# Another fixed order for every step of ScalarE and VectorE, and a Sqrt as the first activation

## What is computed

```
# first block, layer 0 (T = 16 meta tokens + 256)
proj = rmsnorm(h) @ w_in                        # latents q (3 tiles), kv (2), rotary key, gate (8 tiles)
q  = rmsnorm(q_lat)  @ w_uq ; kv = rmsnorm(kv_lat) @ w_ukv
y  = causal_attention(q, kv) * silu(gate)       # 8 heads; silu by tanh on the chip
h += y @ w_out
# layer 1: gated linear recurrence
u, gate = split(rmsnorm(h) @ w_in); uc = conv4(u)
r, i = sigmoid(uc @ w_rg + b), sigmoid(uc @ w_ig + b)
log_a = -8 * r * softplus(-lam); a = exp(log_a); b = sqrt(-expm1(2 log_a)) * i * uc
h += (scan(a, b) * silu(gate)) @ w_out ; x = rmsnorm(h)
# second block, layers 0 and 1: attention over tokens and over a memory, then a squared-ReLU MLP
x += concat(attention, memory_attention) @ w_out ; x += relu(rmsnorm(x) @ w_up)**2 @ w_down
return rmsnorm(x)
```

## Time and profile before

| | us |
|---|---|
| median of 3 runs | 815.59 (815.41 to 815.99) |
| span of the profiled execution | 814.4 |
| TensorE (PE) busy | 801.8, 98% |
| VectorE (DVE) busy | 602.5, 74% |
| ScalarE (ACT) busy | 550.7, 68% |
| granted TensorE clock, mean | 0.998 |

### The profile page before, as it was taken

How to read it: one execution, slowest core, us unless ns; L and a number is a source line. 1 busy time by engine, 2 the same in 40 slices (tenths; PEclk the granted TensorE clock), 3 DMA queues, 4 the chain that set the end, 5 groups by cost and what they waited for, 6 DMA issues and landing times.

```text
span 814.4 us, 14821 instructions
## 1 busy us (share of the span) xinstructions
PE 801.8 (98%) x5854; PEld 747.8 (92%) x5854; DVE 602.5 (74%) x1140; ACT 550.7 (68%) x1045; POOL 0.2 (0%) x4
## 2 busy tenths in 40 slices
PE   8999999999999999999999999999999999999997
PEld 8989899999999899988989999998899888888886
DVE  7999997989987995876657475866757667564664
ACT  7876876699977888767455465668866756553652
POOL 0000000000000000000000000000000000000000
PEclk9999999999999999999999999999999999999999
DMA  9533344665564544464837365444434657554451
GB/s 329 191 103 130 105 147 144 201 201 169 182 202 130 175 137 130 155 226 137 281 117 248 130 238 178 130 133 153 149 111 157 211 177 236 188 175 167 166 181 52
DMA packets 40676, 137.83 MB, mean 169 GB/s; under 512 B 4640, under 2 KB 6176, under 8 KB 40608
## 3 DMA queue, kind: packets, MB, share of 16 engines
q1 hardware_dynamic: 39600, 135.70, 50.0%
q10 hardware_dynamic: 1008, 1.20, 0.4%
HBM read 135.83 MB, written 1.05 MB: 168 GB/s over the span
## 4 chain that ended last, share of the span: by engine, by line
PE 88%; DVE 9%; ACT 1%; issue 1%; DMA 1%; ACTq 0%; DVEq 0%
PE bank L796 15%; PE bank L803 15%; PE bank L798 14%; PE bank L797 14%; PE bank L804 7%; PE bank L807 5%; PE bank L809 5%; PE bank L808 5%; DVE weights_lo L1753 2%; PE bank L1171 2%; DVE temp L1753 1%; DMA weights_raw<-stream_dram 1%; DVE arena L1753 1%; DVE operand L1753 1%; DVE temp L1756 1%
## 5 line engine op out<-in xcount | busy, mean ns | idle before, releaser
L1753 DVE TENSOR_TENSOR weights_lo<-weights_raw,weights_hi 128x1024 fp32r<-128x1024 f32 (+3 forms) x257 | 299.7, 1191 | 37.1 <-ACT weights_hi L1249 36.7
L796 PE MATMUL bank<-operand,weights_hi 128*128 128x256 f32 (+1 forms) x1092 | 313.5, 287 | 1.6 <-DVE weights_lo L1753 1.0
L798 PE MATMUL bank<-operand,weights_lo 128*128 128x256 f32 (+1 forms) x1092 | 309.5, 283 | 0.0
L797 PE MATMUL bank<-operand,weights_hi 128*128 128x256 f32 (+1 forms) x1092 | 309.1, 283 | 0.0
L1249 ACT ACTIVATE weights_hi<-weights_raw 128x1024 fp32r<-128x1024 f32 (+3 forms) x257 | 257.3, 1031 | 76.2 <-PE bank L798 34.6
L796 PEld LDWEIGHTS bank<-operand,weights_hi 128*128 128x128 f32 x1092 | 206.1, 189 | 7.6 <-issue 5.0
L798 PEld LDWEIGHTS bank<-operand,weights_lo 128*128 128x128 f32 x1092 | 206.2, 189 | 0.0
L797 PEld LDWEIGHTS bank<-operand,weights_hi 128*128 128x128 f32 x1092 | 205.8, 188 | 0.0
L803 PE MATMUL bank<-operand,weights_hi 128*128 128x512 f32 x512 | 180.1, 394 | 0.0
L804 PE MATMUL bank<-operand,weights_lo 128*128 128x256 f32 x512 | 143.6, 281 | 0.0
L803 PEld LDWEIGHTS bank<-operand,weights_hi 128*128 128x128 f32 x512 | 96.2, 188 | 21.3
(11 more groups left out here) (212 smaller groups left out, 791.8 us busy)
## 6 DMA issues: line engine op xcount, KB each, us to landing
weights_raw<-stream_dram SPq DMA_DIRECT2D x242, 512.0 KB, 4.3
weights_raw<-stream_dram SPq DMA_DIRECT2D x6, 384.0 KB, 3.5
temp<-memT_dram SPq DMA_DIRECT2D x8, 256.0 KB, 5.2
weights_raw<-stream_dram SPq DMA_DIRECT2D x6, 256.0 KB, 5.7
residual<-xT_dram SPq DMA_DIRECT2D x6, 136.0 KB, 5.5
constants<-consts_dram SPq DMA_DIRECT2D x1, 536.5 KB, 6.9
arena<-consts_dram SPq DMA_DIRECT2D x1, 512.0 KB, 4.3
out_dram<-arena SPq DMA_DIRECT2D x2, 256.0 KB, 2.5
```

The source lines that it names most:

```text
L796: e.matmul(to, w_h, x_h, start=start, stop=False, skip_group_check=True)
L797: e.matmul(to, w_h, x_l, start=False, stop=False, skip_group_check=True)
L798: return e.matmul(to, w_l, x_h, start=False, stop=stop, skip_group_check=True)
L1753: return e.tensor_tensor(to, a, b, op)
```

## The change

Every row of `TIMES` except a few entries has new numbers, so ScalarE's and VectorE's lists are sorted otherwise; TensorE's list, SyncE's list and the set of instructions stay. Some rows (old, then new):

```diff
-    ("scalar", "root"): (9.33, 13.18, 13.27, 31.5, 35.75, 73.33, 101.33, 167.33, 192.67),
+    ("scalar", "root"): (7.5, 13.2, 13.4, 34.2, 36.5, 73.5, 99.667, 165.333, 193.667),
-    ("scalar", "small"): (8.5,),
+    ("scalar", "small"): (13.8,),
-    ("scalar", "lambda_exp"): (17.5,),
+    ("scalar", "lambda_exp"): (30.667,),
-    ("scalar", "rotated_hi"): (13.91, 18.57, 22.12),
+    ("scalar", "rotated_hi"): (12.5, 19.143, 20.875),
-    ("vector", "rstd"): (8.75, 13.13, 13.07, 31.33, 36.25, 71.5, 99.5, 164.2, 191.5),
+    ("vector", "rstd"): (6.5, 13.222, 13.167, 32.111, 35.5, 71.5, 99.667, 162.857, 192.333),
-    ("vector", "small"): (4.5, 8.25, 8.5, 9.2, 40.2, 15.83),
+    ("vector", "small"): (4.5, 13.333, 15.3, 19.533, 33.5, 56.545),
...
-                    copy(cols[:, 21:22], EPS_COL, scale=1.0)
+                    e.activation(cols[:, 21:22], EPS_COL, ACT.Sqrt, bias=0.0, scale=1.0)
```

More of the change, by code:

```diff
@@ L239 @@
[L239 to L253, removed]
@@ L280 @@
[L280 to L292, removed]
@@ L293 @@
[L293 to L298, removed]
-    ("vector", "softmax_norm"): (74.56, 74.33, 74.78, 74.89, 166.5, 167.43, 167.71, 167.57, 171.33, 172.8, 173.17,
-        173.5, 174.62, 174.5, 175.5, 176.5, 180.62, 180.75, 181.75, 181.5),
@@ L320 @@
-    ("vector", "add_up"): (99.25, 99.75, 103.33, 104.33, 104.67, 106.8, 107.5, 108.17, 108.33, 108.83, 109.5,
[4 rows of a table removed]
-    ("vector", "total_out"): (250.25, 249.5),
-    ("vector", "gain_out"): (250.5, 250.75),
+    ("scalar", "root"): (7.5, 13.2, 13.4, 34.2, 36.5, 73.5, 99.667, 165.333, 193.667),
+    ("scalar", "row"): (9.25, 14.25, 14.625, 34.6, 39.5, 78.333, 74.5, 103.5, 165.667, 197.1),
+    ("scalar", "latent_hi"): (14.5, 14.875, 14.75, 15.667, 15.333),
+    ("scalar", "meta_latent"): (18.25, 17.75),
@@ new lines @@
+    ("scalar", "small"): (13.8,),
+    ("scalar", "lambda_exp"): (30.667,),
+    ("scalar", "mla_softmax"): (19.571, 20.25, 20.625, 21.333, 23.667, 26.333, 26.667, 28.083),
+    ("scalar", "mla_turned"): (20.125, 20.75, 21.667, 23.833, 24.75, 27.333, 28.417, 28.5),
+    ("scalar", "mla_y"): (20.5, 23.167, 24.5, 27.667, 28.333, 28.583, 28.75, 28.833),
+    ("scalar", "memory"): (28.167, 28.917, 29.2, 29.8, 48.75, 48.25, 50.5, 56.4),
+    ("scalar", "taps"): (45.25, 42.333, 44.5, 43.5, 47.333, 47.667, 51.25, 51.5),
@@ new lines @@
+    ("scalar", "inputs"): (49.333, 51.75, 58.667, 60.125),
+    ("scalar", "inputs_root"): (56.6, 56.8, 60.625, 60.75),
+    ("scalar", "silu_gates"): (58.333, 61.5),
+    ("scalar", "y_b"): (60.5, 60.25, 60.375, 60.875, 63.5, 63.75, 63.25, 62.5),
+    ("scalar", "softmax"): (75.5, 75.75, 77.5, 77.333, 81.25, 81.5, 82.375, 82.25, 87.429, 87.143, 87.857,
+        87.714, 90.333, 90.667, 91.286, 91.571, 168.2, 168.4, 169.25, 169.75, 171.333, 171.444, 173.125, 173.25,
+        178.286, 178.429, 179.091, 178.571, 182.667, 182.333, 183.273, 183.454),
@@ new lines @@
+    ("vector", "mla_mask"): (17.5, 18.75, 19.4, 19.667, 21.5, 23.6, 24.222, 25.375),
+    ("vector", "mla_norm"): (18.25, 19.267, 19.8, 20.5, 23.4, 24.778, 24.889, 25.875),
+    ("vector", "mla_turned"): (19.2, 19.6, 20.167, 23.2, 24.333, 25.5, 26.133, 26.267),
+    ("vector", "mla_y"): (19.333, 20.333, 21.25, 24.556, 25.75, 26.067, 26.6, 26.667),
+    ("vector", "mla_y_rest"): (19.467, 20.833, 24.667, 25.125, 26.4, 26.467, 26.8, 26.867),
+    ("vector", "memory"): (26.733, 26.933, 27.25, 28.5, 48.167, 48.25, 53.5, 56.182),
@@ new lines @@
+    ("vector", "taps"): (39.571, 39.429, 39.857, 40.2, 43.5, 44.5, 48.75, 48.833),
+    ("vector", "conv_rest"): (42.8, 40.8, 42.6, 40.6, 48.417, 48.333, 48.917, 49.5),
+    ("vector", "inputs"): (48.083, 48.667, 56.091, 56.455),
+    ("vector", "inputs_square"): (50.5, 52.5, 58.857, 60.077),
+    ("vector", "inputs_mult"): (56.636, 58.286, 60.615, 60.692),
+    ("vector", "scan"): (56.909, 56.818, 58.429, 59.667, 61.143, 60.769, 61.286, 60.846),
+    ("vector", "y_b"): (58.143, 58.714, 59.333, 60.154, 61.857, 61.571, 61.714, 61.429),
@@ new lines @@
+    ("vector", "y_2"): (78.667, 80.75, 170.25, 171.5, 174.667, 177.5, 178.667, 179.5, 184.333, 184.667),
+    ("vector", "scale_x"): (76.571,),
+    ("vector", "merge"): (78.333, 80.25, 86.182, 86.546, 88.333, 88.833),
+    ("vector", "sub_mean"): (84.5, 89.5, 93.5),
+    ("vector", "sub_norm"): (86.636, 93.25, 93.75),
+    ("vector", "sub_turn"): (88.667, 94.333, 94.667),
+    ("vector", "evacuate"): (9.125, 9.375, 9.875, 9.75, 13.056, 12.5, 13.389, 15.2, 15.5, 19.133, 20.667, 25.25,
[7 rows of a table added]
+    ("vector", "finish"): (9.25, 9.625, 13.111, 13.278, 13.444, 13.944, 15.4, 19.067, 15.1, 15.8, 15.7, 15.6,
[5 rows of a table added]
@@ L327 @@
+    ("vector", "add_up"): (99.333, 103.333, 103.667, 104.8, 104.4, 106.25, 106.75, 107.5, 107.667, 108.333,
[5 rows of a table added]
+    ("vector", "total_out"): (248.5, 249.333),
+    ("vector", "gain_out"): (251.5, 249.667),
 }
```

51 lines of the change are left out of this document (26 added, 25 removed), and 56 rows, old and new, of the table TIMES.

## The result

| | us |
|---|---|
| kernel before, median of 4 runs | 815.66 (815.41 to 815.99) |
| changed kernel, median of 4 runs | 820.30 (819.52 to 822.52) |
| ratio | 1.0055, 95% interval 1.0044 to 1.0067 |
| profiled execution of the changed kernel | 819.77, span 818.0 |

What follows compares the result with a forecast made beforehand. DVE's work and waits were taken to bound 20 to 113 us. Exit +0.1, later stages +0.1 and an allowance of -0.2 left the span at 814.4; with 1.2 us run overhead, 815.5 us was forecast, range 814.6 to 816.4.

Steps and rivals of the forecast that it cites:

- part 1 and 5: DVE's work up to unit 24's last input: 0.4 us saved by moving small 5; exit sum taken as +0.1 us.
- as before: Inside the heads: DVE's order of masks, norms and the tail from norm 7 on was taken as unchanged.
- First root (2): First root and spread: PE's 1.41 us wait goes, a new DVE wait of 0.9 us comes, latents start at 27.3.
- Roots ahead of the tanhs (3): Up to 45 us: ACT's table loads fall from five to two; new DVE wait of 0.8 us at gate 6's product.
- the loads stay: Rival: the Sqrt table doesn't last from the start, first root 1.3 us later, 816.9 us; chance 0.04.
- Keys first (4): Unit 15: keys before rotary queries remove PE's waits of 0.5 and 0.3 us and most of DVE's 0.61 us.
- Behind 113 us (6): From 113 us on: PE waits under 1 us, DVE and ACT have room to follow; sum +0.1 us.
- The one place that I priced there: Second block, layer 1, rotary copy at 568.81: later behind exponentials and scalings, costed at +0.4 us, bounds 0 and 0.9.
- slower by late copies: Rival: second block, ACT hands back rotary copies later, 0.9 us per layer, 817.2 to 817.5 us; chance 0.13.
- an allowance of -0.2 us: Whole kernel: some 0.2 us taken off the span for an order whose last steps fit a little better.
- no PE wait up to 240 us: Test of the forecast: after unit 24's last input, within 0.8 us of 112.07, PE has no wait until 240 us.

Runs made afterwards that it cites:

- e7: Kernel before with small steps 1 to 5 and two exponentials put behind the heads: 820.29 us, ratio 1.0046.
- e13: Kernel before with changed order below step 26, Sqrt, changed second-block layer 1 attention, small steps in idle places behind the heads: 814.13 us, ratio 0.9977.
- e12: Changed kernel with the old Copy in place of the Sqrt as first activation: 821.03 us, ratio 1.0055.
- e16: Changed kernel with DVE's conversion 33 put ahead of unit 31's evacuation and finish: 819.57 us, ratio 1.0047.
- e5: Kernel before with the changed order for steps 156.5 to 188 only (second block, second layer's attention): 814.21 us, ratio 0.9978.
- e3: Kernel before with the changed order for steps from 68 on only (second block): 817.70 us, ratio 1.0018.
- e14: Kernel before with changed order from 36.3 to 46 (row b behind conversion 39) and convolution 7's low part behind conversion 49: 816.17 us, ratio 1.0002.
- e10: Kernel before with changed second-block layer 1 attention, small steps in DVE's idle places and exponentials moved later: 813.36 us, ratio 0.9965.
- e2: Kernel before with the changed order for steps 26 to 67 only, small series and Copy as before: 829.83 us, ratio 1.0172.
- e17: Kernel before with changed order from 36.3 to 46, unit 31's finish ahead of DVE's conversion 33 and small 4 behind it: 817.19 us, ratio 1.0013.
- e1: Kernel before with the changed order below step 26, changed small steps and late exponential, and Sqrt: 817.84 us, ratio 1.0020.
- e4: Changed kernel with six numbers altered to put needed steps first near the memory norm, row b and convolution 7: 818.96 us, ratio 1.0035.
- e9: Kernel before with changed order up to unit 15, Sqrt, small 4, 5 and late exponential behind old-order heads, changed second-block attention: 814.60 us, ratio 0.9984.

## Why the prediction was wrong

1. **DVE's budget (part 1 and 5): result right, reason half right.** Exit of the heads +0.1 predicted, +0.23 measured behind the start; PE 2.6 us ahead at 62 us, as said. From the first mask on DVE runs without a wait in both kernels, and its work sets the exit. But ahead of that "how much DVE work lies ahead" isn't the measure: e7 took away 4.5 us and got 1.46, as the rest turned into waits for PE and ACT. And the order inside the heads isn't quite "as before": it brings a DVE wait of 0.9 us, which small 3 covers in the changed kernel and e13 lays bare.
2. **First root (2): right.** Wait 0.98 for 0.9, latents at 27.71 for 27.3, spread without a wait.
3. **Roots ahead of the tanhs (3): right,** 0.6 us for 0.8, two loads. The Sqrt's own part is nothing (e12), which also answers the rival "the loads stay" : with the load back in place, its 1.3 us didn't arise.
4. **Keys first (4): right.** Both waits at unit 15 are gone.
5. **Behind 113 us (6): this step failed,** +0.1 predicted and +3.03 measured. "DVE and ACT have room to follow" was read from shares of busy time and from a short list of PE's waits, and neither says in which order a list does its work. I followed both lists to the last `mla_y_rest` and not beyond. The term of +0.1 priced one place and left out three others up to 240 us. At row b (+1.07) and convolution 7 (+1.08) needed steps had moved behind conversions while DVE's conversion 33 had moved back; with that one put forward (e16) the two stretches lose 0.23 and 0.25. At the memory norm (+0.69) DVE has a new wait for ACT of 0.79 us at 116 us. The second block adds +0.28, +0.82 and +0.81. The one place that I priced there, the rotary copy at 568.81, had the wrong sign: the stretch around it is 1.72 us shorter (e5). The rival "slower by late copies" had the right side with the wrong place and 817.5 at most. The total also held an allowance of -0.2 us for "last steps that fit a little better", for which no row stood; behind 700 us the two traces stay the same distance apart.
6. The statement "no PE wait up to 240 us" named the test that this step failed.
7. Not settled: the memory norm's +0.7, which is read from the traces but which no run took away, and the +1.6 in the second block at 300-535 and 575-700, which e3 shows as a stretch and no run divides; that late sums of DVE (L808) cause them is argued from the waits only.

## What to carry to other kernels

A short list of waits in a program of fixed lists means a lead, not room: compare the old and new lists over the whole program, and for each step that moved back ask what now stands ahead of it and when that is released, through buffers and transfers too. An order that is harmless alone can cost a microsecond in a list that is late for another reason (e14 against e16 and the changed kernel), so price pairs, and run each half alone. Put fillers where the trace shows the engine idle, and not ahead of a step that TensorE waits for: 4.3 us or nothing (e7, e10).

## What the runs showed of the hardware

- A wait can be worth something. With the old early order and the full clock the stretch 20-62 lies within 0.03 us of the kernel before (e2, e3, e17). In e5 and e14 PE was granted half its clock for a time at the start (0.57 from 8 to 12 us) and came 1.0 to 1.2 us late. DVE's reciprocal was not late with it (27.17 and 27.36 us, where the kernel before has 27.56), so the wait of 1.41 us at the first spread took the delay up (-1.38 in e5, -1.43 in e14). The new order has no such wait and paid it in full (e1, e4: late by 1.53 and 1.00 at the start, and then -2.77 and -2.76, as with a punctual start). The clock isn't the only cause of a late start: e9 came 2.19 late with 1.00 from 8 to 12 us. From 8 to 12 us, in e5:

```profile
8.00:12.00 4.00, 4.00 (x21) 3.76 (x20) 3.84 (x8) 3.78 (x9) 0.00 (x0) 0.57 1.07 398
```

- With the new order of the heads and the small steps ahead of them, the clock fell behind the turns at 80 us in three of six traces (0.74, 0.86, 0.89 from 84 to 90 us) and the heads took 0.9 us more each time (+3.88 or +3.89 for +2.99 or +3.00); with the old order of the heads in none (eleven traces). The waits ahead were the same in all six, so what decides is not shown.
- Products on 64 rows of two heads run side by side or not, and the view of busy time hardly tells: from 530 to 580 us PE is busy 49.54 us in the kernel before and 49.89 in e5, but with 404 and 418 products.
